# Building the gates between the U products in a two-block network's expert layer, with one-hots on ScalarE and more gather slots

## The chip, the cores and the metric

The kernel runs on one core of one Trainium2 chip. The metric is the device time of one execution in microseconds (us), as the median over runs. All arithmetic here is in fp32.

## What is computed

The whole kernel is a small network of two blocks (256 tokens of width 1024, plus 256 context tokens). The change touches one layer, the expert layer (PEER) of the first trunk layer in the second block, which is applied to the tokens and to the context tokens:

```python
def peer_ffn(h, wq, sub_keys, eu, ev):          # per token t
    q = (t @ wq).reshape(TOKEN_BLOCK, PEER_HEADS, 2, PEER_DK // 2)
    s = jnp.einsum("thpd,hpnd->thpn", q, sub_keys)
    st, it = lax.top_k(s, PEER_TOPK)            # 16 of 128 keys per half
    ...
    best, pos = lax.top_k(cand, PEER_TOPK)      # 16 of the 16 x 16 pairs
    e = jnp.take_along_axis(cidx, pos, axis=-1) # expert = row key * 128 + column key
    g = jax.nn.softmax(best, axis=-1)
    u = jnp.take(eu, e, axis=0)
    act = jax.nn.gelu(jnp.einsum("thkd,td->thk", u, t), approximate=False)
    return jnp.einsum("thk,thkd->td", g * act, jnp.take(ev, e, axis=0))
```

There are 8 heads with 16 picks each, so 128 experts per token out of 128 x 128 = 16384, with rows of 1024 in the tables U and V.

## The kernel before

The layer treats its two streams of 256 tokens in two ways, side by side in one phase.

**Dense stream (the tokens), on TensorE.** For all 16384 experts the products with U are made: 128 blocks c (`up(c)`), each 8 matmuls of 128x128 by 128x256 into one of the PSUM banks 4 to 7; the experts of one block share their row key c. ScalarE takes each through Gelu into row c of the big tile S (`gelu(c)`, line 2434). Then the gates: for each token t, TensorE multiplies two one-hot matrices, hotA (which row key each of the token's 128 picks has) and hotB (which column key, times the softmax weight), and gets the token's 128x128 gate matrix. A quad q is four tokens (`build(q)`, line 2346), one PSUM bank of 0 to 3; there are 64 quads. VectorE makes hotA for a quad in one instruction (`hit_rows`, line 2591) and two of the four hotB (line 2595); ScalarE makes the other two (`weighted_keys`) as Abs(iota - column) and then Relu(weight - weight x distance) (lines 2423 and 2428). VectorE multiplies the gates into S (`gate(q)`, line 2602), over all 128 rows and four tokens. Last come the products with V: 128 blocks (`down(c)`, line 2354), each 4 matmuls of 128x128 by 128x512, summed over all c in the banks 0 to 3, which are the banks of the gates too. The two one-hot buffers alternate.

**Sparse stream (the context), by gathers.** GpSimd issues 512 indirect DMAs (line 2292), each of which fetches one row of U or V for 128 tokens (512 KB) into one of the four slots of the tile G. The order is 128 U rows and 128 V rows for the first 128 tokens, then the same for the others. VectorE spends each in one step (`spend`): a product with a sum for a U row (line 2491), a weighted addition for a V row (line 2497). Step j frees the slot for gather j + 4. Steps are put by hand between the other work of VectorE: among the instructions of the top-16 searches until step 128, then in a row until `BEFORE = 250`, then one behind each gate, then all that are left.

**Order.** TensorE's queue holds all U products, with the turning of the found indices (`turn_found`) behind up(85), then all 64 builds, then, after the last gate, all V products. ScalarE's queue holds the Gelus 0 to 81, the copies of the found indices (`keep_found`), a Gelu of the first picks, the Gelus 82 to 127, then the one-hots. SyncE streams U and V blocks (512 KB each) through a ring of six slots (line 254); a slot is free when its product is done. The phase ends when every engine is through; the next one (from line 2652 on) begins with transposes on TensorE.

The second trunk layer has the same expert layer for the tokens alone, and there the gates are built between the U products from row 50 on (`gelu_late`, lines 2966 and 2968, `keep_rest`, line 2975, the gate, line 3105, `gate_late`, line 3111, the build, line 2828). That code is not touched.

Of the kernel before, what the change touches and what calls it, by code (L numbers as in the profile page):

```python
# [176 lines left out]
def build(nc, x, smalls, consts, mix_tables, tables, axial, w_in1, w_lru, w_br, w_o1, w_f1, w_f2, ada, w_in2,  # L177
          w_out2, w_q2, keys2, peer_u, peer_v, u_rows, v_rows, lam, out):
    ctx = ExitStack()
    with ctx:  # L180
# [1273 lines left out]
        for l in range(LAYERS):  # L1454
# [772 lines left out]
            if not last:  # L2227
# [8 lines left out]
                neg = A.take(T)  # L2236
                flat = S.rearrange("p c t -> p (c t)")
# [23 lines left out]
                BEFORE = 250  # L2261
                n0 = used[0]
                u0, v0 = 16, 16 + NK

# [3 lines left out]

                with Phase("keys_in", "by_q", "n_normed", "n_high", "xt_ps", "a_xt", "s_ps", "a_s", "v_read", "v_diff", "a_e",
                           "a_far", "v_idx", "v_found", "t_ps", "a_t", "v_chain", "a_gelu", "a_col", "v_hot",  # L2270
                           "g_ps", "v_g", "spent", "a_act", "g_in0", "g_in1", "g_in2", "g_in3") as (
                        block, keys_in, by_q, n_normed, n_high, xt_ps, a_xt, s_ps, a_s, v_read, v_diff, a_e,
                        a_far, v_idx, v_found, t_ps, a_t, v_chain, a_gelu, a_col, v_hot,
# [8 lines left out]
                    @block.gpsimd  # L2282
                    def _(pool):
                        def gather(j):
                            n, k = divmod(j, 2 * PICKS)
                            rows = u_rows if k < PICKS else v_rows
                            c = n * PICKS + k % PICKS
                            if k == 0:
                                pool.wait_ge(v_idx, n + 1)
                            if j >= NH:  # L2290
                                pool.wait_ge(spent, j - NH + 1)
                            pool.indirect_dma_start(  # L2292
                                G[:, j % NH, :], None, rows,
                                bass.IndirectOffsetOnAxis(ap=idx_u[:, c:c + 1], axis=0)).then_inc(g_in[j % NH], 16)

                        for j in range(STEPS):
                            gather(j)

                    @block.tensor
                    def _(pe):  # L2300
# [39 lines left out]
                        def build(q):  # L2340
                            pe.wait_ge(v_hot, q + 1)
                            pe.wait_ge(a_col, q + 1)
                            if q >= 4:
                                pe.wait_ge(v_g, q - 3)
# [28 lines left out]
                        for c in range(NK):  # L2373
                            up(c)
# [15 lines left out]
                    def _(act):  # L2390
# [20 lines left out]
                        def keep_found(n):  # L2411
                            act.wait_ge(t_ps, n + 1)
                            act.activation(rows_[:, n * P:(n + 1) * P], bank[0][:, 0:128], ACT.Copy)
                            act.activation(cols_[:, n * P:(n + 1) * P], bank[0][:, 128:256], ACT.Copy)
# [3 lines left out]
                        def weighted_keys(q):  # L2418
                            if q >= 2:
                                act.wait_ge(g_ps, q - 1)  # L2420
                            for u in range(2):
                                t = 4 * q + u
                                act.activation(hotB[:, q % 2, u, :], cc("iota"), ACT.Abs, bias=cols_[:, t:t + 1],
                                               scale=-1.0).then_inc(a_far, 1)
                            for u in range(2):
                                t = 4 * q + u
                                act.wait_ge(a_far, 2 * q + u + 1)
# [49 lines left out]
                    def _(dve):  # L2477
# [4 lines left out]
                        def spend():  # L2482
# [5 lines left out]
                            rows = G[:, j % NH, :].rearrange("p (a t) -> p a t", a=4)  # L2488
                            dve.wait_ge(g_in[j % NH], 16 * (j // NH + 1))
# [97 lines left out]
                        def hit_rows(q):  # L2587
                            if q >= 2:
# [3 lines left out]
                                              rows_[:, r].unsqueeze(2).to_broadcast([P, 4, P]), ALU.is_equal)  # L2592
# [4 lines left out]
                            ins.then_inc(v_hot, 1)  # L2597

                        def gate(q):
                            dve.wait_ge(g_ps, q + 1)  # L2600
                            w = S[:, :, 4 * q:4 * q + 4]
                            dve.tensor_tensor(w, w, bank[q % 4][:, :].rearrange("p (t k) -> p k t", t=4),  # L2602
                                              ALU.mult).then_inc(v_g, 1)

# [9 lines left out]
                        while step[0] < BEFORE:  # L2614
                            spend()
# [740 lines left out]
```

## Time and profile before

| | before |
|---|---|
| median of 3 runs | 3429.46 us (3414.82 to 3431.39) |
| the profiled execution | 3425.08 us, its span 3423.2 us |
| granted TensorE clock, mean | 0.933 |
| TensorE busy (PE) | 3111.7 us, 91% of the span |
| VectorE busy (DVE) | 2355.1 us, 69% |
| ScalarE busy (ACT) | 1121.3 us, 33% |
| GpSimd busy (POOL) | 1057.5 us, 31% |
| HBM traffic | 219 GB/s over the span |

The profile names the engines PE (matmuls), PEld (weight loads), DVE, ACT, POOL and SP. The layer of the change runs from about 1040 to 2354 us of the span. Shares over the whole span say little here: the layer has stretches with different limits. Each fp32 matmul shows as two records. Times in the rows are microseconds unless marked ns. In a row of a timeline, "[6.00 <-X]" means that the engine sat idle for 6 us before it and that X ended the wait; x3 means three instructions in one line, whose duration is that of all of them.

### The profile page before, as it was taken

What the parts mean: (1) busy time and instruction counts of PE and PEld (TensorE: products, weight loads), DVE (VectorE), ACT (ScalarE), POOL (GpSimd) and SP (SyncE); (2) the same over time, 40 slices, a digit from 0 to 9 for tenths busy, and PEclk for the clock granted to TensorE, in tenths of its full rate; (3) what the DMA queues carried; (4) which work ended last, traced back from release to release, by engine and by line L of the source; (5) the groups of instructions that cost most, each with busy time, mean ns of one, the idle gap of its engine ahead of it and who ended that gap; (6) DMA issues with size and microseconds to landing.
All of it is one profiled execution on the core that took longest, in us unless ns stands there. A gap on an engine that the chain in (4) does not pass through costs nothing. (4 is left out here: it accounts for less than half of the span.)

```text
span 3423.2 us, 48390 instructions
## 1 busy us (share of the span) xinstructions
PE 3111.7 (91%) x17340; PEld 2550.8 (75%) x17340; DVE 2355.1 (69%) x4543; ACT 1121.3 (33%) x2140; POOL 1057.5 (31%) x712
## 2 busy tenths in 40 slices
PE   9999999999989999388067999998989999999998
PEld 8788889987778888377056444445878999998887
DVE  7554647668745999755699655555774988975555
ACT  5344424543422111011045100002544444444554
POOL 4556118300000344645643545443004930000000
PEclk9999999999989999789555899998989999999999
DMA  7666855531123899899866899995314544445554
GB/s 272 226 235 233 297 188 194 168 131 65 50 81 135 305 338 330 305 349 386 272 193 181 319 388 389 385 380 206 107 47 149 180 158 148 147 156 194 192 194 139
DMA packets 211819, 754.16 MB, mean 220 GB/s; under 512 B 23456, under 2 KB 29216, under 8 KB 211616
## 3 DMA queue, kind: packets, MB, share of 16 engines
q1 hardware_dynamic: 135184, 480.59, 40.1%
q0 software_dynamic: 73728, 268.47, 22.1%
q8 instruction: 129, 2.11, 0.2%
q10 hardware_dynamic: 2704, 2.38, 0.2%
q14 instruction: 74, 0.61, 0.1%
HBM read 748.20 MB, written 1.05 MB: 219 GB/s over the span
## 5 line engine op out<-in xcount | busy, mean ns | idle before, releaser
L2292 POOL DMA_INDIRECT ring_hi<-in_u_rows,arena x256 | 293.2, 1145 | 748.7 <-DVE arena L2583 385.2
L275 PE MATMUL bank<-H,ring 128*128 128x256 f32 x2304 | 500.9, 380 | 5.5 <-ACT arena L2434 2.8
L275 PEld LDWEIGHTS bank<-H,ring 128*128 128x128 f32 x2304 | 438.7, 191 | 66.7 <-ACT arena L2434 3.2
L2497 DVE SCALAR_TENSOR_TENSOR H<-ring_hi,arena,H 128x1024 f32<-128x1024 f32 x254 | 326.6, 1286 | 222.7 <-DMA ring_hi<-in_v_rows,arena 219.5
L2354 PE MATMUL bank<-ring,arena 128*128 128x512 f32 x1024 | 442.1, 595 | 1.4 <-DVE arena L2602 1.4
L290 POOL TENSOR_TENSOR ring_r<-ring,ring_hi_r 128x1024 fp32r<-128x1024 f32 x133 | 321.2, 2417 | 362.5 <-ACT ring_hi_r L284 362.4
L2491 DVE CUSTOM_DVE_ANT_1 ring_hi<-ring_hi,H 128x1024 f32<-128x1024 f32 x256 | 318.0, 1246 | 101.8 <-DMA ring_hi<-in_u_rows,arena 100.3
L2354 PEld LDWEIGHTS bank<-ring,arena 128*128 128x128 f32 x1024 | 195.4, 191 | 247.5 <-issue 245.8
L2292 POOL DMA_INDIRECT ring_hi<-in_v_rows,arena x256 | 291.6, 1139 | 274.5 <-DVE H L2497 243.1
L284 ACT ACTIVATE ring_hi_r<-ring 128x1024 fp32r<-128x1024 f32 x235 | 247.4, 1056 | 299.1 <-PE bank L302 247.0
L2908 ACT ACTIVATE ring_hi_r<-ring 128x1024 fp32r<-128x1024 f32 x260 | 275.4, 1059 | 167.4 <-PE bank L2846 167.2
L2789 PE MATMUL bank<-H_r,ring_hi_r 128*128 128x256 f32 x1072 | 309.1, 288 | 2.2 <-POOL ring_r L2774 2.2
L300 PE MATMUL bank<-H_r,ring_hi_r 128*128 128x256 f32 x1056 | 307.1, 291 | 3.1 <-PEq L318 1.8
L2791 PE MATMUL bank<-H_r,ring_r 128*128 128x256 f32 x1072 | 303.1, 283 | 0.0
L2790 PE MATMUL bank<-H_r,ring_hi_r 128*128 128x256 f32 x1072 | 303.1, 283 | 0.0
L301 PE MATMUL bank<-H_r,ring_hi_r 128*128 128x256 f32 x1056 | 298.7, 283 | 0.0
L302 PE MATMUL bank<-H_r,ring_r 128*128 128x256 f32 x1056 | 298.6, 283 | 0.0
L2346 PE MATMUL bank<-arena 128*128 128x128 f32 x512 | 131.5, 438 | 156.1 <-DVE arena L2595 156.1
L2346 PEld LDWEIGHTS bank<-arena 128*128 128x128 f32 x512 | 113.1, 325 | 174.6 <-issue 107.2
L300 PEld LDWEIGHTS bank<-H_r,ring_hi_r 128*128 128x128 f32 x1056 | 202.3, 192 | 34.4 <-issue 26.4
L2774 POOL TENSOR_TENSOR ring_r<-ring,ring_hi_r 128x1024 fp32r<-128x1024 f32 x52 | 144.1, 2799 | 226.3 <-ACT ring_hi_r L2908 226.3
L2789 PEld LDWEIGHTS bank<-H_r,ring_hi_r 128*128 128x128 f32 x1072 | 205.3, 192 | 2.9 <-ACT arena L2913 1.5
(505 smaller groups left out, 6480.9 us busy)
## 6 DMA issues: line engine op xcount, KB each, us to landing
ring<-in_peer_u SPq DMA_DIRECT2D x256, 512.0 KB
ring<-in_peer_v SPq DMA_DIRECT2D x256, 512.0 KB
ring<-in_w_in SPq DMA_DIRECT2D x135, 512.0 KB
arena<-in_ada SPq DMA_DIRECT2D x96, 512.0 KB, 5.5
ring<-in_w_f SPq DMA_DIRECT2D x72, 512.0 KB
ring<-in_w_br SPq DMA_DIRECT2D x24, 512.0 KB
ring<-in_w_out SPq DMA_DIRECT2D x24, 512.0 KB
ring<-in_w_q SPq DMA_DIRECT2D x24, 512.0 KB
```

What stands on the lines that cost most here:

```text
L275: mm = pe.matmul(out_ap, col(n, kt), rhs(kt), start=(kt == 0), stop=(kt == KT - 1))
L290: eng.tensor_tensor(ring_lo[:, slot, :], ring[:, slot, :], ring_hi[:, m % NH, :].bitcast(F32), ALU.subtract).then_inc(lows, 1)
L300: pe.matmul(o, hi[:, k], x_hi(kt), start=(kt == 0), stop=False)
L301: pe.matmul(o, hi[:, k], x_lo(kt), start=False, stop=False)
L302: mm = pe.matmul(o, lo[:, k], x_hi(kt), start=False, stop=(kt == KT - 1))
L2292: pool.indirect_dma_start(G[:, j % NH, :], None, rows, bass.IndirectOffsetOnAxis(ap=idx_u[:, c:c + 1], axis=0)).then_inc(g_in[j % NH], 16)
L2354: mm = pe.matmul(bank[2 * t + e][:, :], S[:, c, t * P:(t + 1) * P], ring[:, (n0 + v0 + c) % NS, e * 512:(e + 1) * 512], start=(c == 0), st ...
L2491: ins = dve.tensor_tensor_reduce(rows, rows, tokens(n), 1.0, 0.0, ALU.mult, ALU.add, act_[:, c:c + 1])
L2497: ins = dve.scalar_tensor_tensor(tokens(n), rows, act_[:, c:c + 1], tokens(n), ALU.mult, ALU.add)
L2789: pe.matmul(o, hi[:, k], x_hi_[:, kt, :], start=(kt == 0), stop=False)
L2790: pe.matmul(o, hi[:, k], x_lo_[:, kt, :], start=False, stop=False)
L2791: mm = pe.matmul(o, lo[:, k], x_hi_[:, kt, :], start=False, stop=(kt == KT - 1))
```

## The change

The gates are built from row G0 = 88 on, between the U products. Quad q belongs to the U block `first_row[q]` = 88 + q x 40 // 64, so each of the last 40 blocks has one or two quads ahead of it. Rows of S below that block are multiplied by the gate at once (`gate`, now with fewer rows); of the rows from there on, ScalarE copies the gates themselves into S (`keep_rest`), and when the Gelu of such a row comes, it goes to a small tile `late` (four rows) for the tokens that have gates already, and VectorE multiplies the two (`gate_late`). A new tile `late` of 4 x 256 is taken from the arena. All four weighted one-hots of a quad are made by ScalarE, two quads ahead. The V products begin when the last copy and the last late product are done. The gather steps are placed anew: up to step 134 before the gates, one behind each gate and one behind each row, 104 in all, the others after them. From gather 242 on (`MORE_SLOTS`), which waits for the last build and the last late product, seven slots are used: the four of G, the two one-hot tiles and `late`.

```diff
-                BEFORE = 250
+                G0 = 88
+                first_row = [G0 + q * (NK - G0) // QUADS for q in range(QUADS)]
+                FIRST = PICKS + 6
+                MORE_SLOTS = FIRST + QUADS + NK - G0 + NH
+                slots = [G[:, i, :] for i in range(NH)]
+                slots += [hotA.rearrange("p a b c -> p (a b c)"), hotB.rearrange("p a b c -> p (a b c)"),
+                          late.rearrange("p a t -> p (a t)")]
...
+                def slot_of(j):
+
+                    return j % NH if j < MORE_SLOTS else (4, 5, 6, *((MORE_SLOTS + i) % NH for i in range(NH)))[(j - MORE_SLOTS) % 7]
...
-                            if j >= NH:
-                                pool.wait_ge(spent, j - NH + 1)
+                            if j == MORE_SLOTS:
+                                pool.wait_ge(g_ps, QUADS)
+                                pool.wait_ge(v_late, NK - G0)
+                            if sharers(j):
+                                pool.wait_ge(spent, sharers(j)[-1] + 1)
...
                             if q >= 4:
-                                pe.wait_ge(v_g, q - 3)
+                                pe.wait_ge(a_rest, q - 3)
...
                         for c in range(NK):
+                            for q in quads_at(c):
+                                build(q)
                             up(c)
...
-                        pe.wait_ge(a_t, TT)
-                        for q in range(QUADS):
-                            build(q)
-                        pe.wait_ge(v_g, QUADS)
+                        pe.wait_ge(a_rest, QUADS)
+                        pe.wait_ge(v_late, NK - G0)
...
                         def weighted_keys(q):
                             if q >= 2:
                                 act.wait_ge(g_ps, q - 1)
-                            for u in range(2):
+                            for u in range(4):
                                 t = 4 * q + u
-                                act.activation(hotB[:, q % 2, u, :], cc("iota"), ACT.Abs, bias=cols_[:, t:t + 1],
-                                               scale=-1.0).then_inc(a_far, 1)
-                            for u in range(2):
+                                act.activation(hotB[:, q % 2, u, :], cc("iota"), ACT.Abs, bias=cols_[:, t:t + 1]).then_inc(a_far, 1)
+                            for u in range(4):
...
+                        def gelu_late(c):
+                            t = 4 * built(c)
+                            act.wait_ge(blocks_done, n0 + u0 + c + 1)
+                            if c >= G0 + 4:
+                                act.wait_ge(v_late, c - G0 - 3)
+                            g = act.activation(late[:, c % 4, 0:t], bank[4 + c % 4][:, 0:t], ACT.Gelu)
+                            if t < T:
+                                g = act.activation(S[:, c, t:], bank[4 + c % 4][:, t:T], ACT.Gelu)
+                            g.then_inc(a_gelu, 1)
+
+                        def keep_rest(q):
+                            act.wait_ge(v_g, q + 1)
+                            f = first_row[q]
+                            act.activation(S[:, f:, 4 * q:4 * q + 4],
+                                           bank[q % 4][:, :].rearrange("p (t k) -> p k t", t=4)[:, f:, :],
+                                           ACT.Copy).then_inc(a_rest, 1)
...
                         gelu_picks(0)
-                        for c in range(FREE, NK):
+                        weighted_keys(0)
+                        weighted_keys(1)
+                        for c in range(FREE, G0):
                             gelu(c)
-                        for q in range(QUADS):
-                            weighted_keys(q)
+                        for c in range(G0, NK):
+                            for q in quads_at(c):
+                                keep_rest(q)
+                                if q + 2 < QUADS:
+                                    weighted_keys(q + 2)
+                            gelu_late(c)
...
                         def hit_rows(q):
...
-                            for u in (2, 3):
-                                t = 4 * q + u
-                                ins = dve.tensor_scalar(hotB[:, q % 2, u, :], cc("iota"), cols_[:, t:t + 1], wts[:, t:t + 1],
-                                                        ALU.is_equal, ALU.mult)
...
                         def gate(q):
+                            f = first_row[q]
                             dve.wait_ge(g_ps, q + 1)
-                            w = S[:, :, 4 * q:4 * q + 4]
+                            dve.wait_ge(a_gelu, f)
+                            w = S[:, 0:f, 4 * q:4 * q + 4]
...
+                        def gate_late(c):
+                            t = 4 * built(c)
+                            dve.wait_ge(a_gelu, c + 1)
+                            dve.wait_ge(a_rest, built(c))
+                            dve.tensor_tensor(S[:, c, 0:t], S[:, c, 0:t], late[:, c % 4, 0:t], ALU.mult).then_inc(v_late, 1)
...
-                        while step[0] < BEFORE:
-                            spend()
                         dve.wait_ge(a_t, TT)
                         hit_rows(0)
                         hit_rows(1)
-                        dve.wait_ge(a_gelu, NK)
-                        for q in range(QUADS):
-                            gate(q)
-                            if q + 2 < QUADS:
-                                hit_rows(q + 2)
+                        while step[0] < FIRST:
                             spend()
+                        for c in range(G0, NK):
+                            for q in quads_at(c):
+                                gate(q)
+                                if q + 2 < QUADS:
+                                    hit_rows(q + 2)
+                                spend()
+                            if c > G0:
+                                gate_late(c - 1)
+                            spend()
+                        gate_late(NK - 1)
```

## Rows read from the trace of the kernel before

**Rows 1.** Windows by stretch: start:end, us, busy per engine (instructions), clock, DMA share, GB/s

```profile
1468.00:1616.00 148.00, 147.32 (x672) 129.00 (x672) 85.74 (x68) 17.12 (x47) 71.69 (x66) 0.98 0.98 375
1630.00:1721.00 91.00, 0.00 (x0) 0.00 (x0) 60.95 (x48) 0.00 (x0) 59.54 (x48) 0.50 0.84 275
1721.00:1904.00 183.00, 131.50 (x512) 113.07 (x512) 181.86 (x377) 90.69 (x248) 67.56 (x63) 0.51 0.62 184
1904.00:2346.00 442.00, 441.32 (x1023) 195.41 (x1024) 247.27 (x270) 0.31 (x1) 220.56 (x197) 0.99 0.99 381
```

**Rows 2.** Timeline of TensorE, 1380 to 1910 us: start us, us, what, idle before

```profile
1468.40 147.32 PE L275 MATMUL bank<-H,ring 128*128 128x256 f32 x672 [2.77 <-ACT arena L2434]
1722.52 3.75 PE L2346 MATMUL bank<-arena 128*128 128x128 f32 x16 [106.80 <-DVE arena L2595]
...
1904.68 5.60 PE L2354 MATMUL bank<-ring,arena 128*128 128x512 f32 x7 [1.41 <-DVE arena L2602]
```

**Rows 3.** Timeline of VectorE, the last gather step

```profile
2352.71 1.28 DVE L2497 SCALAR_TENSOR_TENSOR H<-ring_hi,arena,H 128x1024 f32<-128x1024 f32 x1 [1.61 <-DMA ring_hi<-in_v_rows,arena]
```

**Rows 4.** Timeline, VectorE's work of one quad in the gate stretch

```profile
1802.08 0.76 DVE L2602 TENSOR_TENSOR arena<-arena,bank 128x512 f32<-128x512 f32 x1
...
1802.68 0.77 DVE L2591 TENSOR_TENSOR arena<-CS,arena 128x512 f32<-128x512 f32 x1
...
1803.28 0.68 DVE L2595 TENSOR_SCALAR arena<-CS,arena,SM 128x128 f32<-128x128 f32 x2
1803.79 1.30 DVE L2491 CUSTOM_DVE_ANT_1 ring_hi<-ring_hi,H 128x1024 f32<-128x1024 f32 x1
...
1804.93 0.76 DVE L2602 TENSOR_TENSOR arena<-arena,bank 128x512 f32<-128x512 f32 x1
```

**Rows 5.** Timeline of ScalarE, the first groups of one-hots

```profile
1616.03 0.68 ACT L2423 ACTIVATE arena<-CS,arena 128x128 f32<-128x128 f32 x2
...
1617.38 0.68 ACT L2423 ACTIVATE arena<-CS,arena 128x128 f32<-128x128 f32 x2
```

**Rows 6.** Timeline, 1463 to 1478 us, ScalarE and VectorE

```profile
1467.98 1.19 ACT L2434 ACTIVATE arena<-bank 128x256 f32<-128x256 f32 x4
...
1469.30 4.07 DVE L2497 SCALAR_TENSOR_TENSOR H<-ring_hi,arena,H 128x1024 f32<-128x1024 f32 x3
...
1474.16 0.38 ACT L2434 ACTIVATE arena<-bank 128x256 f32<-128x256 f32 x1 [5.00 <-PE bank L275]
1477.62 0.38 ACT L2434 ACTIVATE arena<-bank 128x256 f32<-128x256 f32 x1 [3.07 <-PE bank L275]
```

**Rows 7.** Timeline of the second trunk layer, 2880 to 2882 us

```profile
2880.42 1.05 PE L2828 MATMUL bank<-arena 128*128 128x128 f32 x8
...
2880.62 0.25 ACT L2966 ACTIVATE arena<-bank 128x96 f32<-128x96 f32 x1 [2.38 <-PE bank L2791]
...
2880.95 1.06 ACT L2908 ACTIVATE ring_hi_r<-ring 128x1024 fp32r<-128x1024 f32 x1
2881.09 0.25 DVE L3111 TENSOR_TENSOR arena<-arena 128x92 f32<-128x92 f32 x1
...
2881.51 0.48 DVE L3105 TENSOR_TENSOR arena<-arena,bank 128x316 f32<-128x316 f32 x1 [0.18 <-PE bank L2828]
...
2881.90 0.34 ACT L2975 ACTIVATE arena<-bank 128x200 f32<-128x200 f32 x1
```

**Rows 8.** Windows of line 2497 alone (steps on V rows): VectorE busy (steps), clock, DMA

```profile
1468.00:1616.00 148.00, 84.70 (x66) 0.98 0.98 375
1630.00:1721.00 91.00, 60.95 (x48) 0.50 0.84 275
```

**Rows 9.** Windows of a few us around changes of TensorE's clock, columns as in rows 1

```profile
1062.00:1068.00 6.00, 3.85 (x30) 3.38 (x30) 0.00 (x0) 2.45 (x5) 0.00 (x0) 1.00 0.41 145
...
1472.00:1475.00 3.00, 3.00 (x14) 2.62 (x13) 1.44 (x2) 0.38 (x1) 2.39 (x3) 0.92 0.89 228
...
1619.00:1622.00 3.00, 0.00 (x0) 0.00 (x0) 2.34 (x2) 0.00 (x0) 1.83 (x3) 0.55 0.98 370
```

More of the change, by code:

```diff
@@ L2236, in build @@
                 neg = A.take(T)
+                late = A.take(4, T)
                 flat = S.rearrange("p c t -> p (c t)")
@@ L2260, in build, with quads_at, built, sharers @@
                 STEPS = TT * 2 * PICKS
-                BEFORE = 250
+                G0 = 88
+                first_row = [G0 + q * (NK - G0) // QUADS for q in range(QUADS)]
+                def quads_at(c):
+                    return [q for q in range(QUADS) if first_row[q] == c]
+                def built(c):
+                    return sum(f <= c for f in first_row)
                 n0 = used[0]
                 u0, v0 = 16, 16 + NK
+                FIRST = PICKS + 6
[3 more added lines that the diff above has]
+                          late.rearrange("p a t -> p (a t)")]
                 def tokens(n):
                     return H[:, 4 * n:4 * n + 4, 0, :]
+                def slot_of(j):
+                    return j % NH if j < MORE_SLOTS else (4, 5, 6, *((MORE_SLOTS + i) % NH for i in range(NH)))[(j - MORE_SLOTS) % 7]
+                def sharers(j):
+                    return [x for x in range(j) if slot_of(x) == slot_of(j)]
+                def landed(j):
+                    return 16 * (len(sharers(j)) + 1)
                 with Phase("keys_in", "by_q", "n_normed", "n_high", "xt_ps", "a_xt", "s_ps", "a_s", "v_read", "v_diff", "a_e",
-                           "a_far", "v_idx", "v_found", "t_ps", "a_t", "v_chain", "a_gelu", "a_col", "v_hot",
-                           "g_ps", "v_g", "spent", "a_act", "g_in0", "g_in1", "g_in2", "g_in3") as (
+                           "a_far", "a_rest", "v_late", "v_idx", "v_found", "t_ps", "a_t", "v_chain", "a_gelu", "a_col", "v_hot",
+                           "g_ps", "v_g", "spent", "a_act", "g_in0", "g_in1", "g_in2", "g_in3", "g_in4", "g_in5", "g_in6") as (
                         block, keys_in, by_q, n_normed, n_high, xt_ps, a_xt, s_ps, a_s, v_read, v_diff, a_e,
-                        a_far, v_idx, v_found, t_ps, a_t, v_chain, a_gelu, a_col, v_hot,
+                        a_far, a_rest, v_late, v_idx, v_found, t_ps, a_t, v_chain, a_gelu, a_col, v_hot,
                         g_ps, v_g, spent, a_act, *g_in):
@@ L2289, in gather @@
                                 pool.wait_ge(v_idx, n + 1)
-                            if j >= NH:
-                                pool.wait_ge(spent, j - NH + 1)
+                            if j == MORE_SLOTS:
[3 more added lines that the diff above has]
+                                pool.wait_ge(spent, sharers(j)[-1] + 1)
                             pool.indirect_dma_start(
-                                G[:, j % NH, :], None, rows,
-                                bass.IndirectOffsetOnAxis(ap=idx_u[:, c:c + 1], axis=0)).then_inc(g_in[j % NH], 16)
+                                slots[slot_of(j)], None, rows,
+                                bass.IndirectOffsetOnAxis(ap=idx_u[:, c:c + 1], axis=0)).then_inc(g_in[slot_of(j)], 16)
                         for j in range(STEPS):
@@ L2413, in keep_found @@
                             act.activation(rows_[:, n * P:(n + 1) * P], bank[0][:, 0:128], ACT.Copy)
-                            act.activation(cols_[:, n * P:(n + 1) * P], bank[0][:, 128:256], ACT.Copy)
+                            act.activation(cols_[:, n * P:(n + 1) * P], bank[0][:, 128:256], ACT.Copy, scale=-1.0)
                             act.activation(neg[:, n * P:(n + 1) * P], bank[0][:, 256:384], ACT.Copy, scale=-1.0)
@@ L2487, in spend @@
                                 pick_weights(n)
-                            rows = G[:, j % NH, :].rearrange("p (a t) -> p a t", a=4)
-                            dve.wait_ge(g_in[j % NH], 16 * (j // NH + 1))
+                            rows = slots[slot_of(j)].rearrange("p (a t) -> p a t", a=4)
+                            dve.wait_ge(g_in[slot_of(j)], landed(j))
                             if k < PICKS:
```

7 lines of the change are left out of this document (3 added, 4 removed).

## The prediction

> **What bounds the kernel now.** I read the stretches first [rows 1]. From 1468 to 1616 us TensorE streams the last 42 U products without a gap (147.3 of 148 us), from 1630 to 1721 it does nothing, from 1721 to 1904 it builds gates at half clock, and from 1904 to 2346 it streams the V products without a gap (441.3 us). VectorE is full only in the third stretch (181.9 of 183 us). So each stretch has a different bound, and only the path through them counts. TensorE's own rows say what ended its idle time: 106.8 us of nothing until a one-hot of VectorE [rows 2], because VectorE first works off gathers up to step 250. The last gathered row is spent at 2354.0 us [rows 3], some 8 us behind the last V product. So two chains end together: TensorE's, and the 512 gathers. Shortening the first alone gains nothing; both must be followed to the end. The DMA engines are busy 0.84 of the second stretch, 0.62 of the third and 0.99 of the fourth, so what room they have lies in the middle two.
>
> **What the change removes.** On TensorE's chain the 288.8 us from the end of the U products (1615.7) to the first V product (1904.7) [rows 2]: idle time, then 64 quads of 2.86 us. One quad of VectorE now is gate 0.60, one-hots of the rows 0.60, two weighted one-hots 0.51, one gather step 1.14 [rows 4]. The 0.51 goes to ScalarE.
>
> **What it adds, before the loop.** ScalarE's group of two Abs and two Relu repeats every 1.35 us [rows 5], so four and four cost 2.70. Two such groups now stand ahead of Gelu 82, for which TensorE waits: 5.4 us, on the path. TensorE then resumes at about 1473.9 and, as now, starts at half clock: Gelu 87 came 9.6 us after Gelu 82 [rows 6], so it comes at 1483, and gate 0 can start at about 1484. The six gather steps before it (up to step 134) are done by then: four rows have landed and go at 1.40 us apiece [rows 6], the other two follow at the pace below.
>
> **The loop over 40 U rows.** 24 rows have two quads, 16 have one. TensorE needs 3.46 us per product [rows 6] and, at full clock, at most 1.05 per quad [rows 7]: 138 + 67 = 205 us. VectorE needs per quad 0.55 (the gate, now 88 to 127 rows high, between the 0.48 of 316 elements [rows 7] and 0.60), 0.60 and 1.20 for the step (1.28 less the overlap seen in rows 4), and per row 0.25 for the late gate [rows 7] and 1.20: 64 x 2.35 + 40 x 1.45 = 208 us. ScalarE needs 2.70 + 0.2 (the rest of a gate, at most the 0.34 of 200 elements [rows 7]) per quad and 0.33 per row for the split Gelu (from its start to the next instruction's [rows 7]): 64 x 2.9 + 13 = 199 us.
>
> No engine alone sets it, but a ring does. The gate of row c waits for Gelu c-1; ScalarE's copy of the rest waits for that gate; behind it on ScalarE's queue stand the one-hots two quads ahead, and behind those Gelu c. With one quad: 0.33 Gelu, 1.0 for its end, the gate and the handing over, 0.2, 2.7: 4.2 us. With two: the second copy finds its gate done, so 0.2 + 2.7 more: 7.1 us. 24 x 7.1 + 16 x 4.2 = 238 us. TensorE builds ahead of each product and waits for those same one-hots, but finishes its product 2 us before ScalarE comes to its Gelu, so it is not in the ring. VectorE has under a microsecond of slack per row, and its steps wait in order for landings. The 104 steps come every 2.4 us, slower than four slots give beside full U products (66 in 148 us) or alone (48 in 91 us, 1.90 each) [rows 1, 8], so few wait; I add 0.15 each, 15 us. Loop: 253 us, V products from about 1738.
>
> **After the loop.** At that point 134 + 104 = 238 steps are done, 274 are left; now 314 are done when the V products start. I keep TensorE at 441 us: end 2179. In that time four slots took 197 gathers, 2.24 us each, with the DMA engines 0.99 busy at 381 GB/s [rows 1]; three more slots find no room beside the weights, so I price them at nothing there (bounds: 2.24, and 1.90, the pace that gathers now have without the weights; the engines' 0.99 puts it next to the first; each 0.1 us less would take 9 more steps into this stretch and 14 us off the end). 274 - 197 = 77 are left when TensorE is done. Alone, four slots took 1.90 us each. A slot turns in 4 x 1.90 = 7.6 us, so seven slots would give 1.09; then VectorE binds at 1.40 [rows 6] or the DMA engines at 0.524 MB / 381 GB/s = 1.38. Bounds 1.40 and 1.90; I take 1.50, near the lower, since the row of four slots shows waiting for slots and not for bandwidth (0.84 busy). 77 x 1.50 = 115.5: the last step ends at 2294 instead of 2354.
>
> The Trainium skill (DMA: Bandwidth & Descriptors, Anatomy of one DMA) gives a software-issued transfer about 2.0 us plus its bytes at 436 GB/s, an estimate of 3.2 us for one gather. By that rule four slots would already outrun VectorE, and extra slots would be worth nothing. The row disagrees: 7.6 us per turn, of which VectorE's step is 1.28. The tail would be 108 us by the page's rule, 8 us less than mine.
>
> **Sum.** 2354 - 2294 = 60 us off the profiled execution of 3425.1 us: 3365. That execution lies 4.4 us under the median of the runs shown, inside their spread, and I leave it so. What follows the phase stays as it was: it starts with TensorE at half clock now too, after an idle stretch of some 8 us. The two gate buffers, the new copies and the SyncE queue (the same 256 loads, in the same order) cost nothing beyond this; U loads come more slowly because the ring's slots come free more slowly.
>
> **Rivals.** (a) The seven slots bring nothing in the tail: 1.90 instead of 1.50, 31 us more, 3396. For it: the queue of descriptors or GpSimd could be what holds 1.90. Against it: the DMA engines had room. 8%.
> (b) The ring does not bind, because quads of a row overlap better than I drew, and VectorE's 208 us do: 45 us less, 3320. Against it: Gelu c stands behind both groups on a strict queue. 8%.
> (c) The ring is longer: each of its hand-overs crosses two engines, and VectorE is often inside a 1.28 us step when it could gate. With 7.8 us per row instead of 6.3 the loop takes 312 us, 3424, which is no change. For it: VectorE's slack per row is smaller than one step. 12%.
> (d) On the other side: TensorE runs the loop at half clock. Now it was granted 0.51 all through the gate stretch although it was busy 131 of 183 us [rows 1], and it lost the full clock within some 3 us of idling at 1616 [rows 9]. A row would then cost 6.9 us (twice 3.46) and a quad 1.8 (131.5 / 64 = 2.05 with its drain, of which some overlaps the product behind it): 40 x 6.9 + 64 x 1.8 = 391 us, 138 more, 3503. It decides from a loop of 313 us on, where the 60 us are gone. Against it: TensorE at half clock has no gaps in this loop (391 us of work), and after the restart at 1468.4 [rows 2] the window from 1472 on was granted 0.92 already [rows 9]; and a stretch with 3.85 of 6 us busy, 2.15 us of it idle, kept 1.00 [rows 9]. 10%.
> The Trainium skill (TensorE: Matmul & The Clock Gate, HAM oscillation) says that a kernel that keeps stopping for its inputs can pay the change of clock again and again; this is the rule against the change, and by it the result would lie between my 3365 and the 3503 of (d). The trace shows both: the kept clock with short gaps, the lost one with long ones.
>
> **Chances.** The forecast 62%, (a) 8%, (b) 8%, (c) 12%, (d) 10%. A difference of 0.5% (17 us) is about what a measurement of this kernel can tell from none. The forecast, (a) and (b) are faster: 0.78. Of (c) ten parts are within 0.5% and two beyond; with (d), slower has 0.12 and no change 0.10. The range goes from 3315, just under (b), to (c), 3425: it holds the tail's bounds and a V pace down to 1.90, and leaves out (d) and the outer sides of (b) and (c).
>
> **What would show it.** Right: Gelu 82 about 5 us later; no idle stretch of TensorE over 3 us between Gelu 87 and the first V product; the first V product near 1738, at clock 1.00 around it; the copy of the rest on ScalarE released by VectorE's gate, and VectorE's gates released by Gelu; V gathers at 2.2 us, then some 77 at 1.5 us with TensorE idle. Wrong: a clock of 0.5 in the loop (d); gather steps in it that wait long for landings, or rows of 7 us and more on average (c); a tail at 1.9 (a); V products that wait for their weights because seven gathers are queued beside them, which I price at nothing.

## The result, and the profile after

The changed kernel took 3304.35 us (median of 4 runs, 3297.98 to 3307.72) against 3427.59 us of the kernel before: a ratio of 0.9645, with a 95% interval from 0.9614 to 0.9675. That is 123 us less, where 60 to 65 had been forecast. The direction came out as forecast; the size forecast was half of what came. A second measurement on another chip gave 3306.68 us and 0.9665 (0.9649 to 0.9680).

The profiled execution took 3297.98 us with a span of 3296.1. First the page of the changed kernel: busy times, and the GB/s in 40 slices.

```profile
PE 3033.9 (92%) x17340; PEld 2488.3 (75%) x17340; DVE 2327.4 (71%) x4455; ACT 1213.6 (37%) x2499; POOL 1141.5 (35%) x712
...
GB/s 277 224 232 231 298 213 187 176 147 84 58 45 135 224 329 336 330 268 325 323 319 419 420 420 420 419 387 82 84 80 161 178 149 146 148 166 191 193 195 136
```

The slices of 419 and 420 are the V products. No slice of the kernel before reached more than 389, and these are the first sign of where the forecast fell short. Next the windows of the changed kernel, which answer to [rows 1]: the wait for the found indices, the gate loop, the V products, the steps left behind them.

```profile
1397.00:1459.00 62.00, 0.46 (x4) 0.22 (x2) 39.73 (x67) 0.79 (x4) 36.65 (x31) 0.54 0.86 284
1478.00:1715.00 237.00, 201.62 (x1153) 180.01 (x1153) 209.05 (x271) 194.16 (x640) 130.57 (x104) 0.99 0.91 318
1715.00:2156.00 441.00, 441.00 (x1023) 195.07 (x1024) 280.23 (x352) 0.31 (x1) 323.60 (x226) 1.00 1.02 416
2158.00:2229.00 71.00, 0.00 (x0) 0.00 (x0) 63.83 (x50) 0.00 (x0) 49.82 (x45) 0.51 0.94 359
```

The loop keeps the clock at 0.99. VectorE is busy 209 us in it and ScalarE 194, where 208 and 199 were worked out, TensorE 202 where 205 were. But beside the V products 226 gathers were issued, not 197, with the DMA engines' share hardly changed (1.02 for 0.99) and 416 GB/s for 381.

TensorE's timeline, beside [rows 2]: the wait for the found indices, the restart at row 86, the first build, the first V product.

```profile
1459.35 0.90 PE L2369 MATMUL bank<-CS,arena 128*128 128x128 f32 x3 [61.88 <-DVE arena L2592]
1468.44 9.55 PE L275 MATMUL bank<-H,ring 128*128 128x256 f32 x32 [8.19 <-ACT arena L2465]
1477.82 1.95 PE L2378 MATMUL bank<-arena 128*128 128x128 f32 x16
...
1714.83 65.41 PE L2386 MATMUL bank<-ring,arena 128*128 128x512 f32 x147 [4.69 <-issue]
```

The 106.8 us of idling and the 64 quads at half clock are gone, and the V products start 190 us earlier. The 8.19 us are the 2.77 of before plus the two groups of one-hots, 5.4 us, as priced. The V products waited for no weights: they are busy for all of their 441 us. And VectorE's last steps, beside [rows 3]:

```profile
2218.37 5.45 DVE L2551 SCALAR_TENSOR_TENSOR H<-ring_hi,arena,H 128x1024 f32<-128x1024 f32 x4
2223.93 4.06 DVE L2551 SCALAR_TENSOR_TENSOR H<-arena,H 128x1024 f32<-128x1024 f32 x3
2228.10 1.28 DVE L2551 SCALAR_TENSOR_TENSOR H<-ring_hi,arena,H 128x1024 f32<-128x1024 f32 x1
```

The last step ends at 2229.4 us instead of 2354.0. Rows without any idle time in brackets say that VectorE is the bound here, at 1.39 us per step; so it is for the last 46 steps, from 2165.6 us on. GpSimd issues its gathers in that stretch at the same 1.39 us (some 1.08 us each with 0.30 us between them), so whether a faster VectorE would have helped was not shown. All but 2.5 us of the gain lie ahead of this point: 124.6 of the 127.1 us between the two profiled executions.

### The profile page after: what moved, and what is told of

Its sections match the earlier page's. It is cut to its first block and busy times, and to the rows that moved or that the text cites. A ratio compares the mean times of both kernels' runs of the same rounds, so it can differ in the third digit from the quotient of the medians.

```text
span 3296.1 us, 48806 instructions
## 1 busy us (share of the span) xinstructions
PE 3033.9 (92%) x17340; PEld 2488.3 (75%) x17340; DVE 2327.4 (71%) x4455; ACT 1213.6 (37%) x2499; POOL 1141.5 (35%) x712
## 5 line engine op out<-in xcount | busy, mean ns | idle before, releaser
L275 PE MATMUL bank<-H,ring 128*128 128x256 f32 x2304 | 507.9, 381 | 10.9 <-ACT arena L2465 8.2
L2324 POOL DMA_INDIRECT ring_hi<-in_u_rows,arena x200 | 261.9, 1310 | 596.2 <-DVE arena L2637 382.3
L2386 PE MATMUL bank<-ring,arena 128*128 128x512 f32 x1024 | 441.8, 594 | 4.7 <-issue 4.7
L2545 DVE CUSTOM_DVE_ANT_1 ring_hi<-ring_hi,H 128x1024 f32<-128x1024 f32 x200 | 244.2, 1224 | 88.1 <-DMA ring_hi<-in_u_rows,arena 86.3
L2324 POOL DMA_INDIRECT ring_hi<-in_v_rows,arena x195 | 245.0, 1256 | 165.1 <-DVE H L2551 133.0
L2551 DVE SCALAR_TENSOR_TENSOR H<-ring_hi,arena,H 128x1024 f32<-128x1024 f32 x194 | 249.5, 1286 | 62.1 <-DMA ring_hi<-in_v_rows,arena 57.8
L300 PEld LDWEIGHTS bank<-H_r,ring_hi_r 128*128 128x128 f32 x1056 | 202.0, 191 | 34.7 <-issue 25.5
L2850 PEld LDWEIGHTS bank<-H_r,ring_hi_r 128*128 128x128 f32 x1072 | 205.3, 192 | 2.9 <-ACT arena L2974 1.5
L2851 PEld LDWEIGHTS bank<-H_r,ring_hi_r 128*128 128x128 f32 x1072 | 205.5, 192 | 0.0
L2852 PEld LDWEIGHTS bank<-H_r,ring_r 128*128 128x128 f32 x1072 | 205.2, 191 | 0.0
```

Source lines behind the costliest of these rows:

```text
L275: mm = pe.matmul(out_ap, col(n, kt), rhs(kt), start=(kt == 0), stop=(kt == KT - 1))
L300: pe.matmul(o, hi[:, k], x_hi(kt), start=(kt == 0), stop=False)
L2324: pool.indirect_dma_start(slots[slot_of(j)], None, rows, bass.IndirectOffsetOnAxis(ap=idx_u[:, c:c + 1], axis=0)).then_inc(g_in[slot_of(j) ...
L2386: mm = pe.matmul(bank[2 * t + e][:, :], S[:, c, t * P:(t + 1) * P], ring[:, (n0 + v0 + c) % NS, e * 512:(e + 1) * 512], start=(c == 0), st ...
L2551: ins = dve.scalar_tensor_tensor(tokens(n), rows, act_[:, c:c + 1], tokens(n), ALU.mult, ALU.add)
L2850: pe.matmul(o, hi[:, k], x_hi_[:, kt, :], start=(kt == 0), stop=False)
```

## Experiments

**Does the extra speed come from the slots? The new order with four slots.**

```diff
-                    return j % NH if j < MORE_SLOTS else (4, 5, 6, *((MORE_SLOTS + i) % NH for i in range(NH)))[(j - MORE_SLOTS) % 7]
+                    return j % NH
```

> The changed kernel with four gather slots to the end (everything else of the change is kept). Theory S (the slots raise what the DMA engines move beside the V products, from 381 to 416 GB/s, and lift the tail to VectorE's pace): V products from about 1715 us as in the changed kernel, 441 us long, DMA share about 1.0 at 381 to 388 GB/s there, some 197 gathers at 2.24 us in them, then 77 to 80 steps at about 1.9 us; the phase ends near 2306 instead of 2229, the whole near 3378 us. Rival R (the higher rate comes from the new order of the work, or from a TensorE that is earlier, and not from the slots): 416 GB/s and 1.95 us per gather as in the changed kernel, only the tail slower, 50 steps at 1.9: 2253, the whole near 3325.

Measured: 3382.1 us, ratio to the kernel before 0.9885 (0.9859 to 0.9910). Windows of the V products and of the tail:

```profile
1728.00:2167.00 439.00, 438.98 (x1023) 194.47 (x1024) 242.63 (x323) 0.31 (x1) 213.12 (x194) 1.00 1.00 384
2170.00:2323.00 153.00, 0.00 (x0) 0.00 (x0) 101.54 (x79) 0.00 (x0) 96.41 (x76) 0.50 0.81 269
```

194 gathers in 439 us, 2.26 each at 384 GB/s, and 79 steps at 1.94 behind them. Everything that the three slots changed is back to the numbers of [rows 1]. The new order alone is worth 37 to 45 us, the slots on top of it some 78. Rival R falls: neither the order nor an earlier TensorE moves the DMA rate. Read this pair with care: the share says 1.00 here and 1.02 with seven slots, and yet 8% more bytes moved with seven. The share of busy time was no limit.

**The slots alone, in the kernel before.** The same `slots` and `slot_of`, with

```diff
+                MORE_SLOTS = BEFORE + QUADS + NH
...
+                            if j == MORE_SLOTS:
+                                pool.wait_ge(g_ps, QUADS)
```

> The kernel before with the seven slots alone: from gather 318 on, once all gates are built, the two one-hot tiles and a new tile join the four slots. Theory S: the V stretch moves about 416 GB/s, gathers at 1.95 us, so the 198 steps left are done in 386 us, 55 us before the last V product; the phase then ends with TensorE at about 2346 instead of 2354, 8 us less: 3419 us. The slots alone are worth next to nothing, and the new order alone about 50 us, so the 123 us are not a sum of the two. Rival R: pace stays 2.24 us, end at 2354, 3427 us.

Measured: 3415.22 us, ratio 0.9980 (0.9965 to 0.9995). Two windows beside the V products, and VectorE's first instruction after its last step:

```profile
1905.00:2291.00 386.00, 383.81 (x895) 171.07 (x895) 249.30 (x276) 0.31 (x1) 274.13 (x197) 0.99 1.01 411
2295.00:2345.00 50.00, 50.00 (x118) 22.05 (x117) 6.36 (x5) 0.00 (x0) 0.00 (x0) 1.00 0.54 192
```

```profile
2354.39 5.97 DVE L2716 SCALAR_TENSOR_TENSOR X<-bank,MODS,X 128x256 f32<-128x256 f32 x15 [50.26 <-PE bank L2671]
```

The gathers do run at 1.96 us here too, and finish 50 us early, for nothing: TensorE's V products now end the phase. So one half of the change alone gives 4 us, the other 37 to 45, both 116 to 123. There are two chains of nearly equal length. The new order takes 179 us off TensorE's (its V products end at 2168 in the run above instead of 2347) but only 31 us off the gathers' (2323 instead of 2354). The slots alone take 50 us off the gathers' and nothing off TensorE's. So the gain is what the gathers' chain loses, up to where TensorE's ends.

**How many slots are wanted? Five.**

```diff
-                    return j % NH if j < MORE_SLOTS else (4, 5, 6, *((MORE_SLOTS + i) % NH for i in range(NH)))[(j - MORE_SLOTS) % 7]
+                    return j % NH if j < MORE_SLOTS else (4, *((MORE_SLOTS + i) % NH for i in range(NH)))[(j - MORE_SLOTS) % 5]
```

> The changed kernel with five slots beside and behind the V products (only the first one-hot tile joins). A slot turned in 4 x 2.24 = 9.0 us beside the weights with four slots and in 4 x 1.9 = 7.6 alone. If the turn stays as long, five slots give 1.8 us beside the weights, which the DMA engines cap at the 1.95 seen with seven, and 1.52 in the tail: V stretch at about 1.97 us, some 224 steps; tail 53 x 1.5 = 80 us; phase end 9 us behind that of seven slots, about 3313 us. Rival: pace grows evenly with the slots (a third of the way from four to seven): 2.14 us, 206 steps beside V, 70 at 1.7 behind: about 3353 us.

Measured: 3322.43 us, ratio 0.9696 (0.9662 to 0.9729). Windows beside the V products and behind them:

```profile
1729.00:2171.00 442.00, 442.00 (x1024) 195.60 (x1023) 275.96 (x349) 0.31 (x1) 253.74 (x221) 0.99 1.02 411
2172.00:2261.00 89.00, 0.00 (x0) 0.00 (x0) 68.23 (x54) 0.00 (x0) 62.56 (x50) 0.52 0.88 312
```

One slot gives nearly all of it beside the weights (221 gathers, 2.00 us each). Behind them 54 steps take 89 us, 1.65 each, where the turn time said 1.5: a slot's turn (the number of slots times the time per gather) grew from 7.6 to 8.2 us. Five do not reach VectorE's 1.39, seven do; six were not tried. The total is 9 us over what the turn theory gave and 30 us under even growth.

**What sets the gate loop? No gather steps in it.**

```diff
-                MORE_SLOTS = FIRST + QUADS + NK - G0 + NH
+                MORE_SLOTS = FIRST + NH
...
                         for c in range(G0, NK):
                             for q in quads_at(c):
                                 gate(q)
                                 if q + 2 < QUADS:
                                     hit_rows(q + 2)
-                                spend()
                             if c > G0:
                                 gate_late(c - 1)
-                            spend()
```

> The changed kernel without gather steps between the gates: the 104 steps of the loop come behind it, so VectorE has 125 us less to do there. Ring theory (the loop is set by Gelu, gate, copy and one-hots on ScalarE's strict queue): V products still start at about 1715 (loop 236 us, at most 8 less). Rival V (VectorE's own work sets it): the loop falls to TensorE's 205 us, V products from about 1684. Either way 274 + 104 steps are left after it: 226 beside the V products, 152 at 1.39 us behind them, end about 2367 (ring) or 2336 (rival), the whole 3434 or 3403 us.

Measured: 3436.93 us (one run). The window of the loop, and what VectorE's gate waited for in it:

```profile
1487.00:1715.00 228.00, 201.24 (x1156) 180.63 (x1154) 82.18 (x167) 193.41 (x640) 0.00 (x0) 1.00 0.28 95
```

```profile
DVE arena L2653 <- ACT arena L2474: 138.6, 38, 4.7
```

VectorE's work falls from 209 to 82 us, and the loop from 237 to 228 (first build 1487.3, first V product 1715.0). So VectorE's work does not set it; the 125 us of steps turn into 138.6 us of waiting for ScalarE's Gelu. With no steps in the loop this is the bare ring, 228 us where 238 were drawn, and the steps with their landings add 9 us to it where 15 were added. Not too much should be read into a few microseconds here: loops with the same work took 237 us in both traces of the changed kernel, 239 with four slots behind it and 244 with five.

The ring itself, in ScalarE's timeline of the changed kernel: Gelu, the copy of the rest, the four Abs and four Relu, and Gelu again.

```profile
1578.49 0.27 ACT L2472 ACTIVATE arena<-bank 128x112 f32<-128x112 f32 x1
...
1579.65 0.25 ACT L2480 ACTIVATE arena<-bank 128x92 f32<-128x92 f32 x1 [0.73 <-DVE arena L2653]
1579.80 1.27 ACT L2455 ACTIVATE arena<-CS,arena 128x128 f32<-128x128 f32 x4
1580.97 1.64 ACT L2459 ACTIVATE arena<-arena,SM 128x128 f32<-128x128 f32 x4
1582.51 0.25 ACT L2472 ACTIVATE arena<-bank 128x116 f32<-128x116 f32 x1
...
1583.66 0.24 ACT L2480 ACTIVATE arena<-bank 128x88 f32<-128x88 f32 x1 [0.73 <-DVE arena L2653]
...
1586.52 0.23 ACT L2480 ACTIVATE arena<-bank 128x88 f32<-128x88 f32 x1
...
1589.35 0.27 ACT L2472 ACTIVATE arena<-bank 128x124 f32<-128x124 f32 x1
```

From Gelu to Gelu a row with one quad takes 4.02 us and a row with two 6.84 us, for 4.2 and 7.1 forecast: 24 x 6.84 + 16 x 4.02 = 228 us, just the loop without steps. In the trace of that run nearly every row keeps this beat: the rows with two quads take 6.78 to 6.88 us, those with one 3.98 to 4.01, only the last two some 4.8 and 4.4. In the row with two quads the second copy has no idle time ahead of it; only the first waits for VectorE's gate.

**One-hots given back to VectorE: two of four.** The two `tensor_scalar` of the kernel before return to `hit_rows`, ScalarE makes two.

> The changed kernel with two of each four weighted one-hots given back to VectorE, as in the kernel before. Ring theory: a group costs ScalarE 1.35 instead of 2.7 us, so the ring is 4.4 us for two quads and 2.9 for one, 152 us in all, and VectorE's work, now 208 + 64 x 0.51 = 241 us, is what binds: the loop takes about 245 us, near the 236 of the changed kernel; 3298 to 3312 us; ScalarE waits where VectorE waited. Rival (hand-overs between engines set the pace whatever either does): a loop clearly under 236 us.

Measured: 3316.72 us (one run). The window of the loop, and the waits in it:

```profile
1485.00:1733.00 248.00, 204.00 (x1149) 181.55 (x1148) 236.79 (x394) 111.93 (x392) 135.42 (x103) 0.99 0.89 305
```

```profile
ACT arena L2481 <- DVE arena L2659: 127.6, 61, 3.7
...
PE bank L2378 <- DVE arena L2650: 38.4, 20, 3.0
```

The loop takes 249 us (1484.5 to 1733.4) and VectorE is busy 237 of 248. The waits have turned round: ScalarE waits 127.6 us for the gate, TensorE 38.4 us for VectorE's one-hots. So VectorE's work is the bound in this split. Moving the other two one-hots to ScalarE shortened the loop by 12 us from this execution to that of the changed kernel, of which up to 7 us can be scatter between executions; the time of this one run lies above all nine of the changed kernel (the highest is 3311.7 us).

**Three of four on ScalarE**, to see whether they meet lower.

> The changed kernel with one of the four weighted one-hots of a quad made by VectorE. Ring theory: the ring falls to 24 x 5.7 + 16 x 3.5 = 193 us and VectorE's 208 + 16 = 224 us become the bound, with some waits: loop about 230 instead of 237 us, 3297 us. Rival: VectorE's waits for landings and for Gelu keep adding what they add in the split with two (249 where its work was 241): loop 235 or more, no gain.

Measured: 3300.07 us, ratio 0.9641 (0.9614 to 0.9668), against 0.9645 and 0.9665 for the changed kernel: no difference that the intervals show. The loop window:

```profile
1479.00:1718.00 239.00, 208.74 (x1152) 185.29 (x1151) 221.29 (x332) 154.80 (x516) 130.09 (x103) 0.96 0.90 313
```

The loop stays at 239 us (1478.8 to 1718.5), as the rival said. VectorE is busy 221 of them, and ScalarE waits 72.8 us for its gate between 1490 and 1710 us, where it waited 34.9 in the changed kernel: what ScalarE saves, it waits for VectorE.

**Two ways to shorten TensorE's 62 us wait for the found indices.** First, the slots that lie idle until then:

```diff
+                    if j < PICKS:
+                        return j % 7
                     return j % NH if j < MORE_SLOTS else (4, 5, 6, *((MORE_SLOTS + i) % NH for i in range(NH)))[(j - MORE_SLOTS) % 7]
```

> The changed kernel with seven slots for gathers 0 to 127 too (the one-hot tiles and the late tile are idle until then), four in the gate loop, seven from 242 on. TensorE waits 62 us for the found indices while VectorE spends the last 34 of the 128 steps at 1.84 us. Slot theory: they come at 1.4 us (the DMA engines' 1.38 to VectorE's 1.23), so that wait shrinks by 15 to 20 us, and as TensorE and the gathers are both behind it, all of it shows: about 3287 us. Rival: the wait there is not for slots (POOL's issue, or the DMA latency of fresh rows): 3304 us.

Measured: 3281.25 us, ratio 0.9580 (0.9560 to 0.9600). The window of the wait, and TensorE's restart:

```profile
1403.00:1444.00 41.00, 0.00 (x0) 0.00 (x0) 35.14 (x61) 0.15 (x1) 28.96 (x26) 0.54 0.94 361
```

```profile
1444.03 0.90 PE L2371 MATMUL bank<-CS,arena 128*128 128x128 f32 x3 [41.71 <-DVE arena L2594]
```

The wait falls from 61.88 to 41.71 us, and the median by 23 to 25. Here more slots shortened both chains at once.

Second, no wait at all: the last weights are computed behind the search, and the first picks' Gelu moves into the loop.

```diff
-                FIRST = PICKS + 6
+                FIRST = 99
+                TURN = min(c for c in range(G0, NK) if FIRST + built(c) + c - G0 + 1 == PICKS) + 1
...
-                        gelu_picks(0)
...
+                            if c == TURN:
+                                gelu_picks(0)
...
-                        while step[0] < PICKS:
-                            spend()
                         shares(2 * TT - 1)
```

> The changed kernel with the last found weights (shares) computed right behind the search and not behind step 128; the Gelu of the first picks moves into the gate loop. This removes TensorE's whole 62 us wait. Theory (two chains, the gathers' being the longer): V products start 59 us earlier, at 1656, but only 203 steps are done then and not 238; 226 go beside the V products, 83 at 1.39 us are left: the phase ends 17 us earlier, about 3287 us. Rival (TensorE's chain sets the end): 60 us earlier, 3245 us.

Measured: 3292.14 us, ratio 0.9613 (0.9594 to 0.9632). TensorE's turn of the indices, and the V products' window:

```profile
1409.07 0.52 PE L2370 MATMUL bank<-CS,arena 128*128 128x128 f32 x3 [0.96 <-ACT SM L2449]
```

```profile
1667.00:2108.00 441.00, 441.00 (x1023) 195.06 (x1022) 280.57 (x353) 0.31 (x1) 327.33 (x227) 0.99 1.02 417
```

TensorE is 48 us ahead of the changed kernel (V products from 1666.3), and the whole gains 12 to 15 us against the two medians of the changed kernel, as the longer chain, the gathers', said (17). The interval lies clear of the second measurement of the changed kernel and overlaps the first. Removing a 62 us hole of the busiest engine is worth less than making 34 gathers 20 us faster: all four runs with seven slots early lie below all four of this kernel.

**The best of them, with Gelus 82 to 85 ahead of the first one-hots.**

```diff
-                        weighted_keys(0)
-                        weighted_keys(1)
                         for c in range(FREE, G0):
+                            if c == FREE + 4:
+                                weighted_keys(0)
+                                weighted_keys(1)
                             gelu(c)
```

> The kernel with seven slots early, and Gelus 82 to 85 put ahead of the first two groups of weighted one-hots on ScalarE's queue (in the changed kernel these 5.4 us stand between TensorE and its next product). Theory: TensorE restarts 5.4 us earlier, gate 0 and everything behind it too, VectorE's wait of 6 us before gate 0 shrinks: phase end 5 us earlier than with seven slots early, about 3276 us. Rival: the gathers bind there, VectorE then waits for landings instead: 3281 us.

> The changed kernel unaltered, on the same chip as the other of this call, so that the two can be compared: 3304 us by its first runs, the other 23 to 28 us less.

Measured: 3273.19 us (5 runs, 3270.54 to 3287.26), ratio 0.9567 (0.9550 to 0.9584); the changed kernel beside it 3306.68 us, 0.9665 (0.9649 to 0.9680). It beats both kernels. Against seven slots early alone (0.9560 to 0.9600) the intervals overlap, so the last edit's own worth is open. TensorE's restart in the trace:

```profile
1445.80 0.90 PE L2371 MATMUL bank<-CS,arena 128*128 128x128 f32 x3 [39.64 <-DVE arena L2595]
1449.47 9.43 PE L275 MATMUL bank<-H,ring 128*128 128x256 f32 x32 [2.77 <-ACT arena L2467]
```

The gap is 2.77 us again. But the profiled execution was the slowest of its five, and in its loop VectorE waited 24.4 us for landings, against 16.4 with seven slots early alone, and the loop took 246 us against 238. So its trace can't tell what the 5.4 us became.

## Why the prediction was wrong

The forecast was 3365 us with a range from 3315; 3304 lies under it. By the steps of the prediction, against the profiled execution (phase end forecast at 2294, measured 2229.4, so 65 us are to be found):

- **Before the loop: right.** Two groups cost 5.4 us on the path. Gate 0 started at 1478.9 and not 1484, because the found indices came 5.4 us earlier than in the trace of before. That is a difference between executions: the other runs with four early slots had them from 1461 to 1470 us.
- **The loop: mechanism right, size 18 us off.** 254 us forecast, 236 measured from gate 0. The ring was drawn 10 us too long, and what the steps add was put at 15 us where the run without steps shows 9 (with the scatter named there).
- **After the loop: here the prediction failed.** The step was "three more slots find no room beside the weights, so I price them at nothing there", with the DMA engines 0.99 busy as its reason. Measured, seven slots gave 226 gathers at 1.95 us for the 197 at 2.24, near the other end of the bounds, and the two runs with the slots taken away or added alone show that nothing else did it. 51 steps were left behind the V products instead of 77, and 26 x 1.50 is 39 us, the largest part. A busy share of 0.99 was read as a limit. That there might be room stood in the same trace, in two lines that the prediction did not weigh: VectorE's 219.5 us of waits for V rows, from the page of before, and the GB/s in 40 slices of its V products, from the view of its DMA queues between 1904 and 2346 us.

```profile
L2497 DVE SCALAR_TENSOR_TENSOR H<-ring_hi,arena,H 128x1024 f32<-128x1024 f32 x254 | 326.6, 1286 | 222.7 <-DMA ring_hi<-in_v_rows,arena 219.5
```

```profile
GB/s 229 397 385 397 411 347 406 386 398 390 359 401 364 400 385 404 374 395 386 402 370 391 378 397 399 372 399 370 384 407 387 384 366 371 387 347 390 380 369 386
```

The waits alone prove nothing: with seven slots VectorE still waits some 158 us for landings beside the V products, for 192 before, and a slot's turn is 7 x 1.95 = 13.7 us, for 9.0. It is the rate that differs. Before, it goes up and down between 347 and 411 GB/s after its first slice; with seven slots it lies flat at 417 to 421 but for its first two, and from five slots to seven the mean rises only from 411 to 416.
- **The tail: right, a little slow.** 1.42 us per step over 73 us for the 1.50 taken: 4 us. The bounds of 1.40 and 1.90 were the right two, as four slots (1.94) and seven (1.39 while rows are there) show. The rule that the prediction drew from the Trainium skill's fit for one transfer (DMA: Bandwidth & Descriptors, Anatomy of one DMA), that slots would bring nothing there, does not hold in the same pair.
- **Behind the phase:** 2.5 us less, within what executions differ.

5 + 18 + 39 + 4 = 66 us, which is the 65 to be found but for rounding. The range was too narrow too: it named 14 us for each tenth of a microsecond of the V pace and claimed to hold 1.90, but one end for the pace and one for the loop at once, which is what came, lay outside. Two readings of the prediction are off by a tenth or two without any weight: the 288.8 us are 289.0 by the rows, and TensorE's restart at 1473.9 is 1473.8.

Of the rivals, (a) fell with the tail. (b) fell too: the loop was shorter than forecast, but VectorE's work did not bind it, since without its steps it still took 228 us. (c) fell with 5.9 us per row. (d) did not come: the clock in the loop was 0.99. Around the restart, two windows of the changed kernel show how quickly it returned:

```profile
1471.00:1474.00 3.00, 3.00 (x10) 2.38 (x10) 1.28 (x1) 0.00 (x0) 1.88 (x2) 0.62 0.97 348
1474.00:1477.00 3.00, 3.00 (x16) 2.64 (x15) 0.00 (x0) 0.39 (x1) 0.00 (x0) 1.00 0.93 332
```

The gaps between the builds that followed in this execution, 0.3 to 1.8 us and mostly one per row with two quads, never lost it. Two signs of being right, no idle stretch of TensorE over 3 us and clock 1.00 around the first V product, failed all the same: TensorE sat idle for 4.69 us ahead of the first V product, and the granted clock was 0.54 from 1712 to 1715 us and 0.50 from 1715 to 1718. That costs some 2 us: these V products took 441.8 us, and 439.7 in the second measurement of the same kernel, where they began at 1.00. And the loop does not always keep the clock. In the second measurement of the changed kernel it fell three times in the loop and came back each time; the first, from its timeline and its windows:

```profile
1540.39 1.13 PE L2378 MATMUL bank<-arena 128*128 128x128 f32 x8 [2.80 <-issue]
```

```profile
1541.00:1544.00 3.00, 3.00 (x12) 2.47 (x11) 3.00 (x5) 2.69 (x9) 2.05 (x3) 0.58 0.93 311
1544.00:1547.00 3.00, 3.00 (x16) 2.62 (x15) 2.80 (x4) 3.00 (x10) 1.22 (x2) 0.86 0.87 284
```

The others followed two gaps of 1.04 and 1.67 us close together and a gap of 2.10 us. That loop still took 237 us, since TensorE is not in the ring, and ahead of its V products TensorE idled 2.04 us. So what the Trainium skill warns of (TensorE: Matmul & The Clock Gate, HAM oscillation), a change of clock paid again and again, showed in part: three times in 40 rows in one execution, in none in the other, and without a price in the loop. The gate stretch of before had gaps of some 0.78 us between its quads and stayed at half clock, but it began there [rows 1].

## What to carry to other kernels

Where two chains end within a few microseconds of each other, price an edit by both: here one half of the change gave 4 us alone, the other about 40, and the two together 120. Do not read the busy share of the DMA engines as a limit: look at the bytes per second in fine slices. As long as the consumer waits for landings and the rate goes up and down instead of lying flat, another buffer is worth a trial, even at a share of 0.99; here that trial, beside the V products and behind them, was worth 78 us. And a strict queue that carries work for two stages ahead (the one-hots) in front of what the next stage waits for (the Gelu) makes a ring, which an experiment that empties the other engine shows in one run.

## What the hardware showed that was not expected

The DMA engines' busy share said 1.00 at 384 GB/s with four gathers and the weight stream in flight, and 1.02 at 416 with seven; in the latter nearly every slice of the stretch stood at 417 to 421 GB/s, in the changed kernel and in the kernel before with seven slots alike. The GB/s of the changed kernel's V products in 40 slices, from the view of its DMA queues between 1715 and 2156 us:

```profile
GB/s 300 403 419 417 421 421 419 419 420 419 421 420 417 420 420 419 421 418 419 421 420 419 419 420 419 421 419 417 421 420 419 421 417 420 421 418 421 418 418 420
```

So some 420 GB/s is the ceiling of this mix as far as these runs show, and the share is full well below it. Five slots reached 411. The Trainium skill (HBM Reference, Specifications) gives a core that streams alone about 425 GB/s, bounded by its DMA engines, and 358 GB/s as its share when its neighbour streams too. The runs agree with the first within 1.5%; the forecast should have set a rate near it, and not the 381 of the stretch, as what the engines can give. What the engines do between packets when the share is full and the rate is not was not tried.
